# Expert blocks in another order: two gate-and-up pieces, two down pieces one block late, two gate-and-up pieces

## The reference, cut to what matters

```python
def expert_block(args):
    xblk, e = args                                   # 128 rows of one expert
    gate, up = jnp.split(xblk @ w13[e], 2, axis=-1)  # (128,1024) @ (1024,1024)
    return (jax.nn.silu(gate) * up) @ w2[e]          # (128,512) @ (512,1024)

yb = lax.map(expert_block, (xb, block_e)).reshape(-1, D)
contrib = yb[dest] * sw[:, None]
return jax.ops.segment_sum(contrib, stok, num_segments=T)
```

## Time and profile before

| | |
|---|---|
| median of 3 runs | 2715.81 (2714.0 to 2715.81) |
| the profiled execution's own time | 2713.93 |
| its span | 2711.8 |
| TensorE busy | 2438.1 (90% of the span) |
| VectorE busy | 1616.0 (60%) |
| ScalarE busy | 1174.5 (43%) |
| GpSimd (POOL) busy | 544.0 (20%) |
| mean granted TensorE clock | 0.956 |

### The profile page before, as it was taken

One profiled execution on the slowest core, in us unless ns is written; L12 is line 12 of the kernel. 1 busy time (PEld: TensorE's weight loads), 2 busy tenths in 40 slices (PEclk: granted clock), 3 DMA queues, 4 the chain that ended last, 5 costly groups with the idle time before them and its releaser, 6 DMA issues. The chain is left out here.

```text
span 2711.8 us, 32410 instructions
## 1 busy us (share of the span) xinstructions
PE 2438.1 (90%) x13028; PEld 1994.9 (74%) x13028; DVE 1616.0 (60%) x2502; ACT 1174.5 (43%) x1480; POOL 544.0 (20%) x309
## 2 busy tenths in 40 slices
PE   6889999999999999999999999999579999999960
PEld 2289888888889889666999988855257777777740
DVE  3336988988988983000133321145758888888869
ACT  0334677667677675000000000000147777777751
POOL 0011221221121120000344411100013223232320
PEclk8979999999999999999999999999789999999985
DMA  7722233233233224212111131121369999999963
GB/s 262 271 67 80 62 96 101 59 95 97 63 90 103 63 82 152 67 39 54 39 47 47 47 102 41 30 89 58 121 213 348 340 350 353 354 347 337 339 218 141
DMA packets 255525, 397.56 MB, mean 147 GB/s; under 512 B 17571, under 2 KB 167723, under 8 KB 255321
## 3 DMA queue, kind: packets, MB, share of 16 engines
q1 hardware_dynamic: 232368, 344.63, 38.6%
q0 software_dynamic: 14080, 34.61, 3.3%
q10 hardware_dynamic: 8928, 16.26, 1.9%
HBM read 364.66 MB, written 48.22 MB: 152 GB/s over the span
## 5 line engine op out<-in xcount | busy, mean ns | idle before, releaser
L1912 PE MATMUL bank<-u_hi,w_pairs 128*128 128x344 f32 x1344 | 446.6, 332 | 9.1 <-DVE u_lo L1290 9.1
L1913 PE MATMUL bank<-u_lo,w_pairs 128*128 128x344 f32 x1344 | 431.2, 321 | 0.0
L1914 PE MATMUL bank<-u_hi,w_pairs 128*128 128x344 f32 x1344 | 431.1, 321 | 0.0
L1651 DVE TENSOR_TENSOR we_parts<-u_whole,we_parts 128x2048 fp32r<-128x2048 f32 x129 | 295.1, 2287 | 60.0 <-ACT we_parts L1131 59.7
L1131 ACT ACTIVATE we_parts<-u_whole 128x2048 fp32r<-128x2048 f32 x129 | 247.1, 1917 | 51.5 <-PE bank L2176 26.3
L1912 PEld LDWEIGHTS bank<-u_hi,w_pairs 128*128 128x128 f32 x1344 | 255.2, 190 | 14.0 <-DVE u_lo L1290 9.3
L760 POOL TENSOR_TENSOR w_pairs<-arena,w_pairs 128x1024 fp32r<-128x1024 f32 x56 | 150.7, 2692 | 545.1 <-ACT w_pairs L923 544.9
L1913 PEld LDWEIGHTS bank<-u_lo,w_pairs 128*128 128x128 f32 x1344 | 254.7, 190 | 3.9 <-issue 3.8
L1914 PEld LDWEIGHTS bank<-u_hi,w_pairs 128*128 128x128 f32 x1344 | 254.5, 189 | 0.0
L2034 PE MATMUL bank<-arena 128*128 128x344 f32 x768 | 222.2, 452 | 0.0
L2174 PE MATMUL bank<-we_parts,x_parts 128*128 128x512 f32 x512 | 209.8, 410 | 3.3 <-DVE we_parts L1651 1.9
(11 more groups left out here) (340 smaller groups left out, 5029.5 us busy)
## 6 DMA issues: line engine op xcount, KB each, us to landing
u_whole<-in_w_moe_dram SPq DMA_DIRECT2D x128, 1024.0 KB, 7.4
arena<-in_w_moe_dram SPq DMA_DIRECT2D x64, 1024.0 KB, 7.5
arena<-in_w_in_dram SPq DMA_DIRECT2D x88, 512.0 KB, 5.4
arena<-in_w_ada_dram SPq DMA_DIRECT2D x12, 2048.0 KB, 11.6
arena<-cum_dram ACTq DMA_DIRECT2D x62, 256.0 KB, 3.1
yb_dram<-arena POOLq DMA_DIRECT2D x8, 1032.0 KB, 5.0
arena<-in_state_ssm_dram SPq DMA_DIRECT2D x16, 512.0 KB, 5.6
out_dram<-arena SPq DMA_DIRECT2D x16, 512.0 KB, 4.5
```

The costliest lines, as they stand in the source:

```text
L1651: dve.tensor_tensor(w_los[v], wraw[slot], w_his[v].bitcast(F32), ALU.subtract).then_inc(wlo_ready, 1)
L1912: pe.matmul(out, hi[:, k, :], u_hi[:, k, at], start=(k == 0), stop=False)
L1913: pe.matmul(out, hi[:, k, :], u_lo[:, k, at], start=False, stop=False)
L1914: last = pe.matmul(out, lo[:, k, :], u_hi[:, k, at], start=False, stop=(k == KD - 1))
```

## The change

Order of the pieces of block n, after: gate-up 0 and gate-up 1 of block n; down 0 and down 1 of block n - 1; gate-up 2 and 3 of block n. The transposes of h stand between gate-up 0 and 1; those of the rows stay ahead of gate-up 2 and of gate-up 3. ScalarE puts the output rows behind high part 5, VectorE puts low part 2 ahead of the remainder of h. Slots 0, 1, 4, 5 hold gate-up pieces and slots 2, 3 down pieces. At the end one more piece is split after the last block's silu.

```diff
@@ SP
             def load_w2(x, expert):
-                sp.dma_start(wraw[1 + x]..., w2_v[...]).then_inc(wraw_landed[1 + x], 16)
+                sp.dma_start(wraw[2 + x]..., w2_v[...]).then_inc(wraw_landed[2 + x], 16)
...
                     for j in range(6):
                         sp.wait_ge(wlo_ready, i * 12 + (6 * b + 5 + j))
-                        if j in (1, 2):
-                            load_w2(j - 1, before)
+                        if j in (2, 3):
+                            load_w2(j - 2, before)
                         else:
-                            load_w13(j, max(j - 2, 0), expert)
+                            load_w13(j, j if j < 2 else j - 2, expert)
...
-            sp.wait_ge(wlo_ready, extra * 12 + (12 * PAIRS - 7))
-            sp.dma_start(wraw[0][:, 0:P], w13_v[:, 0, 0:P]).then_inc(wraw_landed[0], 16)
             for x in range(2):
-                sp.wait_ge(wlo_ready, extra * 12 + (12 * PAIRS - 6 + x))
+                sp.wait_ge(wlo_ready, extra * 12 + (12 * PAIRS - 7 + x))
+                sp.dma_start(wraw[x][:, 0:P], w13_v[:, 0, 0:P]).then_inc(wraw_landed[x], 16)
+            for x in range(2):
+                sp.wait_ge(wlo_ready, extra * 12 + (12 * PAIRS - 5 + x))
                 load_w2(x, expert)
@@ ScalarE
                 w_high(n, 3)
                 w_high(n, 4)
-                out_rows(1 - b, n - 1, n * 6 + 1, stored)
                 w_high(n, 5)
+                out_rows(1 - b, n - 1, n * 6 + 2, stored)
                 x_high(1 - b, n + 1, 0)
...
             h_high(1, extra * 2 + (2 * PAIRS - 1))
+            w_high(extra * 2 + (2 * PAIRS), 3, True)
             out_rows(1, extra * 2 + (2 * PAIRS - 1), extra * 12 + (12 * PAIRS), extra * 16 + (16 * PAIRS))
@@ VectorE
                 h_both(1 - b, n - 1)
+                w_low(n, 2)
                 h_low(1 - b, n - 1)
-                for j in range(2, 6):
+                for j in range(3, 6):
                     w_low(n, j)
...
+            w_low(extra * 2 + (2 * PAIRS), 2)
             h_low(1, extra * 2 + (2 * PAIRS - 1))
-            w_low(extra * 2 + (2 * PAIRS), 2)
+            w_low(extra * 2 + (2 * PAIRS), 3)
@@ TensorE
-                    gate_up(b, n, 0, 0, (0,))
+                    gate_up(b, n, 0, 0).then_inc(wparts_used, 1)
                     turn_h(1 - b, n - 1)
-                    gate_up(b, n, 0, 0, (1,)).then_inc(wparts_used, 1)
+                    gate_up(b, n, 1, 1).then_inc(wparts_used, 1)
                     if not (isinstance(n, int) and n == 1):
                         pe.wait_ge(o_free, n * 2 - 2)
-                    down(1 - b, n - 1, 0, 2, n * 6).then_inc(wparts_used, 1)
-                    down(1 - b, n - 1, 1, 0, n * 6 + 1).then_inc(wparts_used, 1)
+                    down(1 - b, n - 1, 0, 0, n * 6 + 1).then_inc(wparts_used, 1)
+                    down(1 - b, n - 1, 1, 1, n * 6 + 2).then_inc(wparts_used, 1)
                 skip = 0 if first else 2
-                gate_up(b, n, 1, 1 + skip).then_inc(wparts_used, 1)
                 turn_rows(1 - b, n + 1, 0, landed)
                 gate_up(b, n, 2, 2 + skip).then_inc(wparts_used, 1)
                 turn_rows(1 - b, n + 1, 1, landed)
                 gate_up(b, n, 3, 3 + skip).then_inc(wparts_used, 1)
...
```

More of the change, by code:

```diff
@@ L662, in load_w2 @@
             def load_w2(x, expert):
-                sp.dma_start(wraw[1 + x].rearrange("p (k c) -> p k c", k=2),
-                             w2_v[:, ds(expert * 4 + 2 * x, 2), :]).then_inc(wraw_landed[1 + x], 16)
+                sp.dma_start(wraw[2 + x].rearrange("p (k c) -> p k c", k=2),
+                             w2_v[:, ds(expert * 4 + 2 * x, 2), :]).then_inc(wraw_landed[2 + x], 16)
             sp.wait_ge(wo_done, TILES + 1)
             sp.wait_ge(u2_ready, TILES + 1)
-            for x, j in enumerate((0, 3, 4, 5)):
+            for x, j in enumerate((0, 1, 4, 5)):
                 load_w13(j, x, 0)
@@ L1120, in _, with w_high @@
             act.activation(wb, wb, ACT.Exp).then_inc(route_e, 1)
-            def w_high(n, j):
+            def w_high(n, j, last=False):
                 g = slot_no(n, j)
                 first = isinstance(n, int) and n == 0
-                slot = (0, 3, 4, 5)[j] if first else j
-                act.wait_ge(wraw_landed[slot], n * 16 + (0 if slot in (1, 2) else 16))
-                if not (first and j < 3):
+                slot = (0, 1, 4, 5)[j] if first else j
+                act.wait_ge(wraw_landed[slot], n * 16 + (0 if slot in (2, 3) else 16))
+                if last:
+                    act.wait_ge(wlo_ready, g - 2)
+                elif not (first and j < 3):
                     act.wait_ge(wparts_used, g - 2)
@@ L1646, in w_low @@
             def w_low(n, j):
-                slot = (0, 3, 4, 5)[j] if isinstance(n, int) and n == 0 else j
+                slot = (0, 1, 4, 5)[j] if isinstance(n, int) and n == 0 else j
                 v = parts_of(n, j)
@@ L2244, in _ @@
             pe.wait_ge(o_free, extra * 4 + (4 * PAIRS - 2))
-            down(1, extra * 2 + (2 * PAIRS - 1), 0, 2, extra * 12 + (12 * PAIRS)).then_inc(wparts_used, 1)
-            down(1, extra * 2 + (2 * PAIRS - 1), 1, 0, extra * 12 + (12 * PAIRS + 1)).then_inc(wparts_used, 1)
+            down(1, extra * 2 + (2 * PAIRS - 1), 0, 0, extra * 12 + (12 * PAIRS + 1)).then_inc(wparts_used, 1)
+            down(1, extra * 2 + (2 * PAIRS - 1), 1, 1, extra * 12 + (12 * PAIRS + 2)).then_inc(wparts_used, 1)
 _INS = ["x_prompt", "x_sample", "state_ssm", "state_ssm_conv", "state_sc_conv", "c_prompt", "c_sample", "ln_in_g",
```

## The result

The changed kernel takes 2665.82 (median of 4 runs, 2663.41 to 2668.83) against 2715.81 before: a ratio of 0.9819, with an interval of 0.9806 to 0.9831. The profiled execution took 2665.34 against 2713.93, so 48.6 less.

What follows compares the result with a forecast made beforehand. No engine full; TensorE's 18.03 us a block plus waits, mainly 1.45 for h, bound the expert stage. At 18.2 a block, 31 blocks gain 47.3, less 0.8 at the end: 2667.4, plus 1.9 gives 2669; range 2659 to 2690.

Steps and rivals of the forecast that it cites:

- The h chain: Second transposes of x to h on TensorE, 6.09 us; cover grows from 4.64 to 6.01, stall falls 1.45 to 0.08.
- The splits of the later pieces: Low parts on VectorE for down pieces and the next two: 1.0, 0.6, 1.4 and 2 us to spare, priced at nothing.
- The remainder of x ahead of piece 0: Second half of x before the next block's piece 0: ready within 0.1 us of TensorE asking, priced at nothing.
- the stream: TensorE's own work in one expert block, six pieces and three groups of transposes without waits: 18.03 us.
- The 18.1 of the undisturbed block: Expert block after the change: 18.03 us of TensorE work plus 0.08 left waiting for h.
- The bound from below, 17.95: Shortest expert block, in us: TensorE's work with the shorter transposes and no stall.
- The irregularity of 0.1 kept from before: Blocks before ran 19.62 us undisturbed, 19.72 on average; that 0.1 was kept, making 18.2 a block.
- the prediction's own count of 2.4 to spare: Output rows in each block would come about 2.4 us after the scatter's landing.
- The end: After the last silu, both last down pieces are split behind h: 0.8 us lost, once.
- the rival: DMA becomes the expert stage's bound, share rising from 0.96 to 1.00: 18.84 us a block, kernel 2689; chance 0.20.
- Scatter: Rival: output rows wait for the scatter's landing, kernel slower; with a 14.5 us landing 20.3 a block, 2734; chance 0.05.
- moved stall: Rival: h's wait goes but down pieces' splits come as late, a wait of 1.5 us; kernel 2716; chance 0.04.

Runs made afterwards that it cites:

- the swap on VectorE: Kernel after, with the remainder of h put back ahead of the first down piece's low part on VectorE: 2700.87, ratio 0.9942.
- the second: The kernel after, unchanged, run once more to measure its end: 2667.59, ratio 0.9825.

## Why the prediction held, step by step

**The h chain: right.** The cover of 6.01 against a chain of 6.09 was to leave 0.08; the rows show no gap ahead of the transposes of h. The two runs with only one half of the change, the swap on VectorE and the output rows one place earlier show that the moves work only together.

**The splits of the later pieces: right, within 0.2.** VectorE's order of time, with POOL's instructions beside it:

```profile
2204.19 0.69 DVE L1770 TENSOR_TENSOR arena<-arena,bank 128x512 f32<-128x512 f32 x1
2204.79 2.29 DVE L1655 TENSOR_TENSOR we_parts<-arena,we_parts 128x2048 fp32r<-128x2048 f32 x1
2206.99 0.68 DVE L1774 TENSOR_TENSOR x_parts<-bank,x_parts 128x512 fp32r<-128x512 f32 x1
2208.07 4.64 DVE L1655 TENSOR_TENSOR we_parts<-u_whole,we_parts 128x2048 fp32r<-128x2048 f32 x2 [0.39 <-ACT we_parts L1134]
2213.14 2.29 DVE L1655 TENSOR_TENSOR we_parts<-u_whole,we_parts 128x2048 fp32r<-128x2048 f32 x1 [0.43 <-ACT we_parts L1134]
...
2216.40 1.03 POOL L838 DMA_INDIRECT arena<-u_dram,arena  x1 [0.51 <-POOL arena L849]
2217.26 2.29 DVE L1655 TENSOR_TENSOR we_parts<-u_whole,we_parts 128x2048 fp32r<-128x2048 f32 x1 [1.11 <-ACT we_parts L1134]
2217.45 2.15 POOL L849 TENSOR_TENSOR arena<-arena 128x1 f32<-128x1 f32 x1
...
2219.76 1.02 POOL L842 DMA_INDIRECT rows_dram<-arena  x1 [0.16 <-POOL arena L849]
...
2220.07 2.28 DVE L1655 TENSOR_TENSOR we_parts<-arena,we_parts 128x2048 fp32r<-128x2048 f32 x1
```

The first down piece's low part ends at 2207.08 and TensorE starts the piece at 2208.21: 1.1 to spare, forecast 1.0. Half of the 4.64 ends at 2210.39, wanted at 2210.93: 0.5, forecast 0.6. Then 2212.71 for 2214.01 (1.3, forecast 1.4) and 2215.43 for 2217.22 (1.8, forecast 2).

**The remainder of x ahead of piece 0: mis-sized, and hidden by a second error.** "Ready within 0.1 of when TensorE asks", priced at nothing. It costs the gap of 0.15 and another 0.10, because the first matmul after a wait takes 0.50 and the next follows 0.33 behind it instead of 0.23: 0.25 a block. Against that the stream is shorter than 18.03. Transposes that nobody waits for take 0.35 (2205.00 to 2205.35), not 0.41, a figure I took from a row behind a wait; pieces are 2.72, not 2.74. That makes 3 x 2.72 + 3 x 2.86 + 3 x 0.35 = 17.79, and 17.79 + 0.25 is the block to within 0.03. The 18.1 of the undisturbed block was right by two errors of a quarter that cancel, which is luck. The bound from below, 17.95, has no working beside it; the rows give 17.79. Moving the copy of x ahead of the output rows brought back 0.10 of the 0.25; the rest reappeared ahead of h, whose transposes then follow by 0.39 instead of 0.23 (2205.36 to 2205.75 in that run). So the 0.08 forecast ahead of h was about 0.16, and in the kernel after the gap ahead of piece 0 covered it.

**The irregularity of 0.1 kept from before: wrong, it went.** Blocks average 18.06 where I said 18.2; that is 0.14 x 31 = 4.4 us. Before, it came with output rows waiting for the scatter's landing. The longest of those eight waits:

```profile
2447.80 0.60 ACT L1151 ACTIVATE arena<-bank 128x512 f32<-128x512 f32 x1 [2.38 <-DMA rows_dram<-arena]
```

Its block, silu to silu, is the longest of all, 21.22; the eight blocks with such a wait took 19.65 to 21.22, the others after the first 19.55 to 19.68. After, none waits, as the prediction's own count of 2.4 to spare should have told me.

**The end: right in place, short in size.** Forecast 0.8, measured 2.3 in the profiled execution and 0.95 in the second. The first down piece starts 5.0 after the last silu, and 4.9 was forecast; I let half clock cover eight matmuls, and it covered 13 and about seven. These last two errors have opposite signs: -4.4 + 1.5, with 0.9 lost ahead of the stage, is -2.0, and 2667.4 was forecast for 2665.34. That the total came so near is luck in part.

**DMA: right side, wrong margin.** I allowed a tenth, from the 413 GB/s of idle engines. Beside busy engines, over a long stretch, the most seen is 389 GB/s, so the margin is 4%. The share that spoke for the rival (0.96) went to 1.00 without binding: it is 1.00 at 375 GB/s and 1.01 at 389, so it does not show what is left. The Trainium skill's page "DMA: Bandwidth & Descriptors", Specifications, gives about 358 GB/s from HBM to one core, half of what a stack gives its two cores, by which the kernel would have come near 2690 (an estimate). The runs differ, with 375 and 389 GB/s, here with one core at work.

**Scatter and moved stall: right.** Output rows never wait for a landing, which came down from 9.9 to 7.6. The moved stall did not come, but each half of the change by itself is that rival's picture.

## What to carry to other kernels

Where all engines run in a fixed order, write each chain beside the TensorE work that lies between its two ends; a stall goes only when the shortest of those covers exceeds its chain, so moves that are worth little one by one can be worth much together. Within an engine's order, put ahead what has its input and is wanted soon, and behind what waits for another engine. Take a stream's length from rows with no wait in front of them, and count for a wait the slower restart behind it too.

## What was not expected of the hardware

**GpSimd's DMA instructions follow VectorE.** The scatter's instruction took 2.89 before and takes 1.02 now, the gather's 1.03. Before, the scatter was issued at 2219.50, inside a low part that ran from 2219.19 to 2221.49; now both are issued while VectorE is between two low parts (2216.40 before 2217.26; 2219.76 after 2219.55). The landing, counted from the instruction's start, fell from 9.9 to 7.6, most of it in the instruction. The small instruction ahead of the scatter (line 849) now falls inside a low part in its turn: it takes 2.15, to 2219.60, where before it took 0.21. So POOL's busy time fell only from 544.0 to 488.8. No run moved this alone, but the run with output rows one place earlier has both lengths in one block:

```profile
2204.54 2.28 DVE L1655 TENSOR_TENSOR we_parts<-u_whole,we_parts 128x2048 fp32r<-128x2048 f32 x1
...
2204.86 2.86 POOL L838 DMA_INDIRECT arena<-u_dram,arena  x1 [0.51 <-POOL arena L849]
...
2208.11 1.02 POOL L842 DMA_INDIRECT rows_dram<-arena  x1 [0.16 <-POOL arena L849]
...
2208.26 2.29 DVE L1655 TENSOR_TENSOR we_parts<-arena,we_parts 128x2048 fp32r<-128x2048 f32 x1 [0.84 <-ACT we_parts L1134]
```

In that run's expert stage all 31 gathers and 11 of 31 scatters are issued inside a low part, take 2.84 to 2.92 and end 0.9 after it; the other 20 scatters are issued outside and take 1.02. That the length follows VectorE is shown; by what means is not. The Trainium skill's page "SBUF — State Buffer", section "SBUF: two separate sides", says that a VectorE operation with two inputs in SBUF and a GpSimd operation that reads SBUF share one pair of ports, and whichever begins first holds it to its end. These rows agree where VectorE begins first. They do not show VectorE held: the low part that begins at 2220.07, with the scatter under way to 2220.78, takes 2.28 as ever.

**The half clock lasts unequally long.** After the same waits (2.79 and 1.60 here) the same kernel ran 13 matmuls at half clock in one execution and about seven in another. In the run with output rows one place earlier, where TensorE waited 2.8 in each block, the stage's mean clock was 0.90. Its price comes on top of the wait itself: of that run's 4.7 more a block than the kernel after, 2.8 is the wait.
